# Last normalisation of a hybrid attention and mixture-of-experts block: its statistics and its second pass spread over three engines, its weights loaded during the experts

## The reference, cut to what matters

```
def layer_norm(x, g, b):
    xf = x.astype(jnp.float32)
    mu = jnp.mean(xf, -1, keepdims=True)
    var = jnp.mean(jnp.square(xf - mu), -1, keepdims=True)
    y = (xf - mu) * lax.rsqrt(var + LN_EPS)
    return (y * g.astype(jnp.float32) + b.astype(jnp.float32)).astype(x.dtype)
...
    ffn = hierarchical_moe(h, ...)
    h = layer_norm(DN_ALPHA * h + ffn, ln2_g[l], ln2_b[l])
return h[:, N_META:]
```

## Time and profile before

| | us |
|---|---|
| median of 3 runs | 2340.93 |
| the profiled execution | 2339.48 |
| its span, first to last instruction | 2337.8 |
| last stage, from its first load (2281.46) to the end of the span | 56.3 |
| VectorE busy in 2289 to 2333 | 40.74 of 44 |
| ScalarE busy in 2289 to 2333 | 38.75 of 44 |
| GpSimd busy in 2289 to 2333 | 8.16 of 44 |

### The profile page before, as it was taken

One profiled execution on the slowest core, in us unless ns is written; L12 is line 12 of the kernel. 1 busy time (PEld: TensorE's weight loads), 2 busy tenths in 40 slices (PEclk: granted clock), 3 DMA queues, 4 the chain that ended last, 5 costly groups with the idle time before them and its releaser, 6 DMA issues. The chain is left out here.

```text
span 2337.8 us, 35821 instructions
## 1 busy us (share of the span) xinstructions
PE 2118.6 (91%) x11168; PEld 1757.6 (75%) x11168; DVE 1644.5 (70%) x3067; ACT 1483.9 (63%) x2262; POOL 488.9 (21%) x561
## 2 busy tenths in 40 slices
PE   6999999879789999999799965999999999999970
PEld 6798989656478888888688854778888888888860
DVE  5323231267588888888433358989999999999976
ACT  5323241276588888887433324778888887888867
POOL 0112111143123333331000011222222222222221
PEclk9999999989989999999899977999999999999995
DMA  6535352633442222211333317998788779999838
GB/s 208 170 129 186 127 181 89 164 85 96 115 102 75 74 75 73 75 57 72 97 144 142 136 72 271 371 321 270 234 274 274 251 247 356 327 312 298 263 80 305
DMA packets 220554, 420.60 MB, mean 180 GB/s; under 512 B 47913, under 2 KB 97145, under 8 KB 219289
## 3 DMA queue, kind: packets, MB, share of 16 engines
q1 hardware_dynamic: 187760, 316.08, 40.2%
q0 software_dynamic: 31648, 101.89, 15.1%
q10 hardware_dynamic: 1040, 1.31, 0.2%
HBM read 437.68 MB, written 86.39 MB: 224 GB/s over the span
## 5 line engine op out<-in xcount | busy, mean ns | idle before, releaser
L2568 DVE TENSOR_TENSOR moe_w_lo<-fetch_w_raw,moe_w_hi 128x1024 fp32r<-128x1024 f32 x376 | 435.6, 1217 | 13.5 <-ACT moe_w_hi L2497 13.4
L2497 ACT ACTIVATE moe_w_hi<-fetch_w_raw 128x1024 fp32r<-128x1024 f32 x376 | 368.7, 1053 | 69.8 <-DMA fetch_w_raw<-in_w_e_up_dram 35.7
L2622 PE MATMUL moe_ps_gu<-moe_w_hi,moe_xT_hi 128*128 128x512 f32 x736 | 293.0, 398 | 4.5 <-DVE moe_xT_lo L2579 4.5
L2624 PE MATMUL moe_ps_gu<-moe_w_hi,moe_xT_lo 128*128 128x512 f32 x736 | 288.6, 392 | 0.0
L2623 PE MATMUL moe_ps_gu<-moe_w_lo,moe_xT_hi 128*128 128x512 f32 x736 | 288.1, 391 | 0.0
L1600 DVE TENSOR_TENSOR fox_p_lo<-fox_ps_t,fox_p_hi 128x512 fp32r<-128x512 f32 (+4 forms) x352 | 211.0, 610 | 43.0 <-ACT fox_p_hi L1534 42.7
L1534 ACT ACTIVATE fox_p_hi<-fox_ps_t 128x512 fp32r<-128x512 f32 (+4 forms) x352 | 182.1, 536 | 67.9 <-PE fox_ps_t L1671 67.1
L2574 DVE TENSOR_TENSOR moe_d_lo<-fetch_d_raw,moe_d_hi 128x1024 fp32r<-128x1024 f32 x184 | 213.1, 1220 | 10.4 <-ACT moe_d_hi L2505 10.4
L1671 PE MATMUL fox_ps_t<-ident,fox_s 128*128 128x128 f32 (+1 forms) x1216 | 195.4, 275 | 13.7 <-ACT fox_s L1527 13.4
L1587 DVE CUSTOM_DVE_ANT_0 fox_s<-fox_ps_r,fox_ncum 128x512 f32<-128x512 f32 (+4 forms) x352 | 193.4, 566 | 12.9 <-PE fox_ps_r L1656 8.7
L512 ACT ACTIVATE proj_qk_out<-proj_ps_chunk 128x512 f32<-128x512 f32 x52 | 31.1, 598 | 252.9 <-PE proj_ps_chunk L746 252.9
(11 more groups left out here) (346 smaller groups left out, 5128.2 us busy)
## 6 DMA issues: line engine op xcount, KB each, us to landing
fetch_w_raw<-in_w_e_gate_dram SPq DMA_DIRECT2D x192, 512.0 KB
fetch_w_raw<-in_w_e_up_dram SPq DMA_DIRECT2D x192, 512.0 KB
fetch_d_raw<-in_w_e_down_dram SPq DMA_DIRECT2D x92, 1024.0 KB
ahead_raw<-in_w_in_dram SPq DMA_DIRECT2D x24, 1024.0 KB, 5.2
gates_wide<-in_x_dram SPq DMA_DIRECT2D x16, 512.0 KB
h<-gates_wide POOLq DMA_DIRECT2D x16, 512.0 KB, 3.3
gates_wide<-qT SPq DMA_DIRECT2D x32, 256.0 KB, 4.3
mix_h<-h SPq DMA_DIRECT2D x16, 512.0 KB, 3.6
```

Of the source, the lines that this page charges most:

```text
L2497: nc.scalar.activation(w_hi[:, k], w_raw[:, k].rearrange("p j n -> p (j n)"), ACT.Copy).then_inc(gu_high, 1)
L2568: nc.vector.tensor_tensor(w_lo[:, k], w_raw[:, k].rearrange("p j n -> p (j n)"), w_hi[:, k].bitcast(F32), ALU.subtract).then_inc(gu_split, 1)
L2622: nc.tensor.matmul(out, xT_hi[:, slot, k], w_hi[:, k, cols], start=k == 0, stop=False)
L2624: done = nc.tensor.matmul(out, xT_lo[:, slot, k], w_hi[:, k, cols], start=False, stop=k == KT - 1)
```

## The change

In the last stage:

- VectorE takes the statistics of six tiles itself (1, 4, 6, 9, 12, 14): two bn_stats of 512 columns and a bn_aggr (`measure`), one tile ahead of their normalisation. ScalarE has only the Sqrt for these.
- VectorE keeps the reciprocal and the first pass of all 16 tiles, and the second pass of six (0, 3, 5, 8, 11, 15).
- For the ten others (1, 2, 4, 6, 7, 9, 10, 12, 13, 14) ScalarE multiplies by rstd (`stretch`, Copy with a scale, placed in its list behind the statistics of the next tile), and GpSimd adds shift (tensor_tensor) and then issues the store.
- `gain` and `shift` are loaded by SyncE in the experts, at block 2, behind the gate and up weights of block 4, and their buffers live from before the routing stage on.
- ScalarE waits for the result of tile n-4 before the Sqrt too, by a wait on the semaphore of each engine that can have made it.

```diff
             def body(b, slot, use):
                 if not is_block(b, 0):
                     fetch_down(b)
                 fetch_gate_up(b + 2)
+                if is_block(b, 2):
+                    sp.dma_start(last["gain"][:], row_broadcast(t["ln2_g"][0], P)).then_inc(last["const_in"], 16)
+                    sp.dma_start(last["shift"][:], row_broadcast(t["ln2_b"][0], P)).then_inc(last["const_in"], 16)
...
+        def by_vector(n):
+            return n % 8 in (1, 4, 6)
+        def by_pool(n):
+            return n % 8 in (1, 2, 4, 6) or n in (7, 13)
...
         @block.gpsimd
+            pool.wait_ge(const_in, 32)
+            for n in range(TILES):
+                if by_pool(n):
+                    pool.wait_ge(stretched, count(by_pool, n + 1))
+                    nc.gpsimd.tensor_tensor(out[:, slot], out[:, slot], shift[:], ALU.add).then_inc(ready_pool, 1)
+                    pool.wait_ge(ready_pool, count(by_pool, n + 1))
+                else:
+                    pool.wait_ge(ready_dve, n + 1 - count(by_pool, n))
                 pool.dma_start(t["out"][0, n * P:(n + 1) * P, :], out[:, slot]).then_inc(stored[slot], 16)
...
         @block.scalar
+            def roots(n, slot, use):
+                wait_ready(act, n - 3)
+                if by_vector(n):
+                    act.wait_ge(spreads, count(by_vector, n + 1))
+                    nc.scalar.activation(std[:, slot:slot + 1], spread[:, slot, 1:2], ACT.Sqrt, bias=eps[:]).then_inc(rooted, 1)
+                    return
+                (Copy, Square and Sqrt as before)
+            def stretch(n, slot):
+                act.wait_ge(normed, n + 1)
+                act.wait_ge(scaled, n + 1)
+                nc.scalar.activation(out[:, slot], out[:, slot], ACT.Copy, scale=rstd[:, slot:slot + 1]).then_inc(stretched, 1)
+            for n in range(TILES):
+                roots(n, n % 4, n // 4)
+                if n > 0 and by_pool(n - 1):
+                    stretch(n - 1, (n - 1) % 4)
...
         @block.vector
+            def measure(n, slot, use):
+                dve.wait_ge(base_in[slot], 16 * (use + 1))
+                wait(dve, rooted, n - 3)
+                wait(dve, spreads, count(by_vector, n))
+                for half in range(2):
+                    nc.vector.bn_stats(out=stats[:, half], in_=base[:, slot, half * D // 2:(half + 1) * D // 2]).then_inc(pieces, 1)
+                dve.wait_ge(pieces, 2 * count(by_vector, n + 1))
+                nc.vector.bn_aggr(out=spread[:, slot], in_=stats[:]).then_inc(spreads, 1)
...
+            dve.wait_ge(const_in, 32)
+            for n in range(TILES):
+                if n + 1 < TILES and by_vector(n + 1):
+                    measure(n + 1, (n + 1) % 4, (n + 1) // 4)
+                normalise(n, n % 4, n // 4)
+                if not by_pool(n):
+                    finish(n, n % 4)
```

More of the change, by code:

```diff
@@ L2664, in _, with phase_combine @@
             down(2 * pairs - 1)
-def phase_combine(nc, sems, t, route):
+def phase_combine(nc, sems, t, last):
     with ExitStack() as ctx:
         m = Space(nc, ctx, "out", sems)
-        gain = m.sb("gain", [P, D])
-        shift = m.sb("shift", [P, D])
+        gain, shift, const_in = last["gain"], last["shift"], last["const_in"]
         eps = m.sb("eps", [P, 1])
@@ L2690, in phase_combine, with count, wait_ready @@
         normed = m.sem("normed")
-        ready = m.sem("ready")
+        stretched = m.sem("stretched")
+        ready_dve = m.sem("ready_dve")
+        ready_pool = m.sem("ready_pool")
         stored = [m.pool_dma_sem(f"stored{i}") for i in range(4)]
         block = ctx.enter_context(nc.Block())
-        def tiles(engine, body):
-            for n in range(TILES):
-                body(n, n % 4, n // 4)
+        def by_vector(n):
+            return n % 8 in (1, 4, 6)
+        def by_pool(n):
+            return n % 8 in (1, 2, 4, 6) or n in (7, 13)
+        def count(kind, n):
+            return sum(1 for i in range(n) if kind(i))
+        def wait_ready(engine, n):
+            wait(engine, ready_pool, count(by_pool, n))
+            wait(engine, ready_dve, n - count(by_pool, n))
         @block.sync
         def _(sp):
-            def load(n, slot, use):
+            for n in range(TILES):
+                slot, use = n % 4, n // 4
                 wait(sp, normed, n - 3)
                 sp.dma_start(base[:, slot], t["acc"][n * P:(n + 1) * P, :]).then_inc(base_in[slot], 16)
[L2705 to L2709, removed]
         @block.gpsimd
@@ L2756, in body @@
                 nc.vector.scalar_tensor_tensor(out=out[:, slot], in0=out[:, slot], scalar=rstd[:, slot:slot + 1],
[L2757 to L2759 removed]
+                                               in1=shift[:], op0=ALU.mult, op1=ALU.add).then_inc(ready_dve, 1)
+            dve.wait_ge(const_in, 32)
+            for n in range(TILES):
+                if n + 1 < TILES and by_vector(n + 1):
[3 more added lines that the diff above has]
+                    finish(n, n % 4)
 def hybrid_block_kernel(nc, t):
@@ L2807, in hybrid_block_kernel @@
             phase_mix(nc, ctx, ident, t, logits, route, ahead)
+        last_rows = Space(nc, ctx, "last", ctx)
+        last = {"gain": last_rows.sb("gain", [P, D]), "shift": last_rows.sb("shift", [P, D]),
+                "const_in": last_rows.pool_dma_sem("const_in")}
         with ExitStack() as fetched:
```

48 lines of the change are left out of this document (25 added, 23 removed).

## The result

The changed kernel takes 2353.06 us (median of six runs, 2351.59 to 2355.3), the kernel before 2341.28 beside it (2340.2 to 2342.33): the ratio is 1.0051, with a 95% interval of 1.0041 to 1.0062. It is slower by about 12 us. The forecast was 2352.8, and "slower" had 0.72.

What follows compares the result with a forecast made beforehand. The prediction took VectorE's beat of 2.65 us per tile to bound the last stage, with ScalarE just as full. It added 9.1 us there and 2.8 in the experts, 11.9 in all, giving 2352.8 us, range 2341 to 2357.

Steps and rivals of the forecast that it cites:

- The exclusion: Last stage: two-input VectorE passes and GpSimd additions reading SBUF exclude each other; six passes held up, 11.9 us.
- The rest of VectorE's line: Last stage, besides held passes: own work 36.0, ScalarE's order 4.4, load waits 1.2 us; 53.5 with the held passes.
- ScalarE's order: Last stage: stretches stand ahead of statistics VectorE waits for, before tiles 3, 8, 11 and 15; 4.4 us.
- twice waits 0.6 for the load: Last stage: measurements want tiles one tile earlier, so VectorE waits for two loads, each 4.3 us from issue.
- That is all that the earlier weights give: 0.6 us: Start of last stage: with gain and shift loaded earlier, tile 0's first pass starts at 2288.39 rather than 2288.99.
- The experts: Loading gain and shift at block 2 puts all later weights back 2.8 us; bounds 0 and 3.7.
- the two signs that the prediction names: Experts: first block after 1560 starts 2.8 later, and ScalarE's waits for weights are longer by that.
- what comes after is held by TensorE and can't win it back: Experts: the 2.8 us lost while the DMA engines are full stays lost in later blocks.
- The sum: Whole kernel: 9.1 us in the last stage plus 2.8 in the experts, 11.9 slower.
- The first rival: Last stage: a two-input pass doesn't wait for GpSimd; stage -0.3, experts +2.8, 2343.4, no tellable change; chance 0.16.
- the slots of out cover the longer way (...) because the pace of four tiles is now 13 as well: Last stage: four output slots suffice for pass, stretch, addition and store landing, about 13 us with queueing.
- The second rival: Last stage: the balance works, only busy sums count; 6.1 us earlier, 2334.8 or 2337.6; chance 0.12, three quarters faster.

Runs made afterwards that it cites:

- the last edit: Changed kernel with PSUM rows, drain ahead of tile 0, eight buffers and late loads, but rows read from SBUF again: 2352.47 us against 2343.0.
- the execution with the early drain: Changed kernel with GpSimd's drain moved from ahead of tile 12's addition to ahead of tile 0: 2351.41 us against 2353.06.
- the one with late rows: Changed kernel with gain and shift loaded at the end of SyncE's list for the experts instead of at block 2: 2352.06 us against 2353.06.
- the two pairs of traces above: Drain ahead of tile 0 against ahead of tile 12, VectorE reading rows from SBUF: 14.48 and 14.50 us from tile 12's reciprocal against 15.04 twice.
- those two kernels: Changed kernel with VectorE's gain and shift in PSUM, drain ahead of tile 12 or tile 0: 2349.56 and 2348.96 us.
- The PSUM kernel: Changed kernel with gain and shift copied to PSUM by ScalarE and read there by VectorE's passes: 2349.56 us against 2353.06.
- three edits more: On top of rows in PSUM: drain ahead of tile 0, loads at the end of SyncE's experts list, eight buffers per ring: 2343.0 us.
- the loosened kernel: Changed kernel with rows in PSUM, drain ahead of tile 0, loads at the end of SyncE's experts list, eight buffers per ring: 2343.0 us.

## Why the prediction was right, point by point

**The exclusion, the step on which it hung: right, in mechanism, count and size.** Forecast: six passes held up, beside the additions of tiles 2, 4, 7, 10, 13 and 14, 11.9 us. Measured: six, beside just these, 12.3. The rule of the Trainium skill (SBUF — State Buffer, Who interferes with whom) is shown here for just the pair that the earlier trace rows left open: a two-input VectorE pass waits for a GpSimd addition, 3.17 to 3.31 us instead of 1.27. Three experiments make it a cause and not a coincidence: GpSimd writing only, and VectorE with one operand in PSUM, both give passes of 1.27; and the last edit, PSUM against SBUF with all other waits gone, is 9.5 us of the median.

**The rest of VectorE's line: near in sum, the load waits mis-sized.** Forecast 53.5 from the first reciprocal to the end of the last pass; measured 56.04 (2292.10 to 2348.14). The measurements are 1.5 each and its own work about 36, as forecast. ScalarE's order cost 3.8 (forecast 4.4), at two places and not four: 1.16 before tile 3 and 2.60 before tile 15. The mis-sized term is "twice waits 0.6 for the load": 1.2 in the forecast, and 2.33 + 1.75 = 4.1 measured. The estimate of 4.3 us from issue was taken from a load that ran alone; the two late ones (tiles 9 and 12), among stores, came 6.17 and 5.59 after the pass that let them go. The size is not a steady one: in the execution with the early drain the same waits were 0.8, in the one with late rows 1.9. Behind VectorE's last pass the end came after 5.56 us (forecast 5.1).

**A step that was missing: the drain.** The prediction followed four lists and left one instruction of GpSimd's out. It held tile 12's addition by 2.1 us. On VectorE's list that is worth 0.6, by the two pairs of traces above; once the exclusion is gone it is worth 4.0 of the stage, in one execution each; the medians of those two kernels differ by 0.6.

**The early rows in the last stage: mis-sized.** "That is all that the earlier weights give: 0.6 us" was meant for the start alone (from first load to first reciprocal 7.45 before and 6.86 forecast; measured 6.49, so 1.0). In the unsplit stage they also take away the wait for the second tile, and are worth 2.7. The row for it stood in the earlier trace rows.

**The experts: right in direction, the size open between 1.3 and 2.6.** Forecast +2.8. The two kernels that differ in the place alone give 2.6 by their medians (0.8 to 5.3), and the same move in the changed kernel 1.0, which can't be told from either. Of the two signs that the prediction names, the first came with a different size, and the second did not come. The first sigmoid after 1560 starts at 1565.2 instead of 1561.2, and counted from the first block 3.5 later, not 2.8. ScalarE's waits for gate and up weights from 1478 to 1566 are 15.6 us (and 1.3 for down weights), not longer than the 18.1 of the earlier trace rows. And the step "what comes after is held by TensorE and can't win it back" is not what the traces show: two blocks on the 3.5 have become 1.4. At the last block the groups of profiled kernels differ by 1.3, within their scatter.

**The sum.** The stage was 11.75 longer in the profiled execution (forecast 9.1, within its bounds of 6.1 to 12.5), and 10.7 in the one with late rows. With 1.3 to 2.6 for the experts these make 12.0 to 14.4. The median time, +11.8, agrees with the forecast's 11.9 more closely than its terms deserve: the stage came out longer than forecast and the experts probably cheaper, and that the two errors cancel is luck.

**The first rival had a wrong number behind a clear mechanism.** "The engines share after all" was to give a stage 0.3 shorter than before. The PSUM kernel is just that case and its stage is 9.3 longer than before (65.61). The failing step is that "the slots of out cover the longer way (...) because the pace of four tiles is now 13 as well", which the rival took over: that holds while the exclusion slows VectorE, and the changed kernel indeed never waits for a store. At the quicker pace the way of a tile (pass, stretch, addition, store) is longer than four tiles, and the drain is reached with more stores in flight. So removing the largest cost returned 2.5 of its 9.7 us in the stage; three edits more were needed for the rest. **The second rival** (the balance works) is refuted by the loosened kernel: with nothing excluded and nothing short, 57.5 us against 53.6 for the unsplit stage with the same early rows. By medians that kernel's own order costs 5.1 (2343.0 less 2337.88) and the exclusion 9.5 more.

What stays open: whether another order of ScalarE's list would bring the loosened stage under 53.6. It was not tried.

The version to keep is the kernel before with its rows loaded behind the last block's issues: 2337.88, ratio 0.9984 (0.9975 to 0.9992). It is a small gain, 3.3 us, and it is the part of the change that didn't need the split.

## What to carry to other kernels

Before you give GpSimd part of VectorE's elementwise work, look at what each reads: here, where both read two SBUF tensors, an addition and a pass that met ran one after the other, and the busy sums that promised balance were void; with VectorE's second operand in PSUM they overlapped. When you take the largest cost away and little comes back, list the waits again: here store landings and a drain stood right behind it, hardly visible while VectorE was slow. And price a preload by the place it gets in the queue: the same two rows cost 2.6 us (0.8 to 5.3) more in front of weights that are waited for than behind them. Last, before you credit an edit with a shorter stage, see where in the trace the time was won: the early drain's 1.6 us lay for the most part ahead of the drain.

## What the runs showed of the hardware

- Not every VectorE instruction is held up by an addition: twelve bn_stats of one 128x512 SBUF tensor took 0.681 each on average, and the pair at 2297.24, beside an addition, 1.28. A TENSOR_SCALAR with one tensor input was held up in the earlier trace rows. What sets the two apart was not tested; the TENSOR_SCALAR alone goes through 2064 elements per partition in 1.21 us, about twice as many per us as bn_stats or a pass.
- One held pass doesn't fit "who comes first": at 2341.01 it is recorded 0.40 ahead of the addition of 2341.41 and still ends 1.09 after that addition, 3.85 us in all. GpSimd was issuing a store at its start. The kernel with late rows has the same (3.84). The issue alone doesn't do it: with the early drain the same pass (2339.30) starts during an issue (2339.27), but with no addition right behind it, and takes 1.26. Its cause was not tested.
- GpSimd's drain waits until its stores have landed. In the PSUM kernel the store ahead of it, issued at 2325.23, lands after 6.6 us, and the next addition starts at 2332.51, 0.7 later; in the changed kernel the store of 2333.47 lands after 3.6, and the addition starts at 2337.68, 0.6 later.
